# Hybrid attention layer on one core: the compressed branch for four heads at once, the gate product on GpSimd, 640-key scores cut as 384 + 256

## What is computed

```python
s = jnp.einsum('bqhgd,bihd->bhgqi', qblk, kc)            # compressed
valid = cmp_end[None, :] <= t[:, None]
p_cmp = jax.nn.softmax(jnp.where(valid, s, -1e30), axis=-1) * valid
o_cmp = jnp.einsum('bhgqi,bihd->bqhgd', p_cmp, vc)
...
p_slc = jax.nn.softmax(s.reshape(*s.shape[:4], n_sel * SLC_BLOCK), axis=-1).reshape(s.shape)
...
p_win = jax.nn.softmax(jnp.where(mw, s, -1e30), axis=-1)
...
o = g[..., 0:1] * o_cmp + g[..., 1:2] * o_slc + g[..., 2:3] * o_win
```

## Time and profile before

| | |
|---|---|
| time, median of 3 runs | 915.43 us (914.12 to 916.51) |
| the profiled execution | 917.05 us, span 915.2 us |
| TensorE busy, of the span | 855.7 us (93%) |
| VectorE | 516.7 us (56%) |
| ScalarE | 468.8 us (51%) |
| GpSimd | 364.0 us (40%) |

### The profile page before, as it was taken

One profiled execution on the slowest core, in us unless ns is written; L12 is line 12 of the kernel. 1 busy time (PEld: TensorE's weight loads), 2 busy tenths in 40 slices (PEclk: granted clock), 3 DMA queues, 4 the chain that ended last, 5 costly groups with the idle time before them and its releaser, 6 DMA issues.

```text
span 915.2 us, 12680 instructions
## 1 busy us (share of the span) xinstructions
PE 855.7 (93%) x4674; PEld 706.3 (77%) x4674; DVE 516.7 (56%) x1066; ACT 468.8 (51%) x1021; POOL 364.0 (40%) x302
## 2 busy tenths in 40 slices
PE   3999999999999999999889998999988999999994
PEld 3887798898888788777677876777767888887883
DVE  5301359281561704476978998899986026363434
ACT  5311343203232015768878897789976252625432
POOL 1311014517132121643336645254544446463563
PEclk9999979999999999999988999999999999999997
DMA  6342011201111010320000000000006723232339
GB/s 224 87 98 51 13 43 35 58 24 47 36 40 42 23 49 21 83 65 1 1 1 1 1 1 1 1 1 1 1 1 225 247 91 97 77 103 78 96 126 242
DMA packets 38397, 55.68 MB, mean 61 GB/s; under 512 B 11312, under 2 KB 17728, under 8 KB 38336
## 3 DMA queue, kind: packets, MB, share of 16 engines
q1 hardware_dynamic: 37616, 52.78, 19.1%
q0 software_dynamic: 720, 2.10, 1.3%
HBM read 48.58 MB, written 6.29 MB: 60 GB/s over the span
## 4 chain that ended last, share of the span: by engine, by line
PE 73%; DVE 16%; ACT 6%; issue 2%; DMA 1%; POOL 1%; SPq 0%; POOLq 0%; DVEq 0%; ACTq 0%
PE psum L718 47%; DVE pT_lo L1763 5%; PE psum L942 3%; PE psum L805 3%; PE psum L959 3%; PE psum L927 2%; PE psum L926 2%; DVE p_win L1740 2%; PE psum L960 2%; ACT pT_hi L1257 2%; PE psum L762 2%; DVE p_slc L1740 1%; PE psum L683 1%; DVE o_sum L1773 1%; DVE gla_z L1694 1%
## 5 line engine op out<-in xcount | busy, mean ns | idle before, releaser
L1374 POOL TENSOR_TENSOR w_lo<-w_raw,w_hi 128x512 fp32r<-128x512 f32 (+1 forms) x134 | 184.1, 1377 | 378.2 <-ACT w_hi L1065 377.7
L1065 ACT ACTIVATE w_hi<-w_raw 128x512 fp32r<-128x512 f32 (+1 forms) x134 | 82.9, 623 | 325.4 <-PE psum L718 304.5
L1763 DVE TENSOR_TENSOR pT_lo<-psum,pT_hi 128x512 fp32r<-128x512 f32 (+1 forms) x148 | 99.9, 685 | 13.7 <-ACT pT_hi L1257 13.0
L718 PE MATMUL psum<-w_hi,xT_hi 128*128 128x512 f32 x256 | 101.2, 395 | 1.7 <-DVE gla_state_b L1675 1.7
L1257 ACT ACTIVATE pT_hi<-psum 128x512 fp32r<-128x512 f32 (+1 forms) x148 | 86.3, 591 | 32.0 <-PE psum L942 31.3
L1406 POOL TENSOR_SCALAR p_slc<-p_slc,gate_over_sum 128x512 f32<-128x512 f32 (+7 forms) x40 | 66.7, 1678 | 85.4 <-DVE gate_over_sum L1749 85.4
L718 PE MATMUL psum<-w_hi,xT_lo 128*128 128x512 f32 x256 | 100.2, 391 | 0.0
L718 PE MATMUL psum<-w_lo,xT_hi 128*128 128x512 f32 x256 | 100.2, 391 | 0.0
L959 PE MATMUL psum<-pT_hi,v_hi_lo 128*128 128x512 f32 x132 | 62.0, 469 | 15.9 <-DVE pT_lo L1763 14.9
L926 PE MATMUL psum<-kT_hi_hi,qT_hi_lo 128*128 128x512 f32 (+3 forms) x192 | 70.9, 375 | 2.7 <-DVE neg_max L1740 2.5
L1248 ACT ACTIVATE p_slc<-p_slc,neg_max 128x512 f32<-128x512 f32 (+7 forms) x80 | 58.1, 728 | 8.8 <-DVE neg_max L1740 8.4
(11 more groups left out here) (261 smaller groups left out, 1961.3 us busy)
## 6 DMA issues: line engine op xcount, KB each, us to landing
w_raw<-in_w_in SPq DMA_DIRECT2D x56, 256.0 KB, 2.7
w_raw<-in_w_out SPq DMA_DIRECT2D x32, 256.0 KB, 2.7
w_raw<-in_ple_gate SPq DMA_DIRECT2D x32, 256.0 KB, 2.5
x_tok<-in_x SPq DMA_DIRECT2D x8, 512.0 KB, 7.0
h_tok<-in_x SPq DMA_DIRECT2D x8, 512.0 KB, 5.6
out<-h_tok SPq DMA_DIRECT2D x8, 512.0 KB, 5.7
w_raw<-in_ple_proj SPq DMA_DIRECT2D x8, 256.0 KB, 2.5
out<-out_tmp POOLq DMA_DIRECT2D x3, 512.0 KB, 5.6
```

Source lines behind the costliest of these rows:

```text
L718: mm = pe.matmul(out, lhs, rhs, start=(first and n == 0), stop=(final and n == 2))
L1065: act.activation(w_hi(i)[:, 0:w], raw[:, i % RAW, 0:w], ACT.Copy).then_inc(s_whi, 1)
L1374: pool.tensor_tensor(w_lo(i)[:, 0:w], raw[:, i % RAW, 0:w], w_hi(i)[:, 0:w].bitcast(F32), ALU.subtract).then_inc(s_wlo, 1)
L1763: dve.tensor_tensor(PTl[0:n, u % 4], bank(4 + u % TRING)[0:n], PTh[0:n, u % 4].bitcast(F32), ALU.subtract).then_inc(s_plo, 1)
```

## The change

The compressed step is no longer four heads one after the other:

- `KC1` and `KC2` become halves of one tile, so a head's scores are one matmul of 128 columns (64 of the high product, 64 of the low one), and four heads fill one bank (`compressed_scores`).
- `compressed_sum`, VectorE: a `tensor_reduce` over the two halves writes the scores of four heads to SBUF.
- `compressed_mask`, GpSimd, adds the mask; `compressed_max`, VectorE, makes the maxima of the four heads; `compressed_less_max`, GpSimd, subtracts them; `compressed_exponent`, ScalarE, is one exponential without a sum; VectorE sums in `gate_over_sum`; `compressed_scale`, GpSimd, is one product for the four heads.
- In all steps `gate_over_sum` is only the inversion, and the product with the gate is made on GpSimd (`gates`); all scalings wait for it.
- `scaler` of the selected branch is "APAP" for "VPAP".
- Scores of 640 keys lie from column 128 of a pair of banks, so they are cut 384 + 256.
- A compressed step uses the pairs of banks once and not four times (`events`, `bank_pair`, `pair_freed`).
- The planner has the new operations and other assumed durations (0.9 x keys for a score, 3.0 x keys for a scaling on GpSimd, where it had 0.83 and 3.6).

The diff, with "..." where lines are left out (declarations, the lists of kinds, the loops that call the new functions):

```diff
     PTl = sb("pT_lo", [P, 4, 512], F32R, R2 + 8192)
-    KC1 = sb("kcT_hi_hi", [P, NKV, 64], F32R, R6 + 7168)
-    KC2 = sb("kcT_lo_lo", [P, NKV, 64], F32R, R6 + 7680)
+    KC = sb("kcT_hi_lo", [P, NKV, 2, 64], F32R, R6 + 7168)
+    KC1, KC2 = KC[:, :, 0], KC[:, :, 1]
...
-    scaler = ("PPPP", "VPAP", "VPAP")
+    scaler = ("P", "APAP", "VPAP")
...
+    def bank_pair(s, g):
+        return event_of[s, g] % 2 * 2
...
+    def pair_freed(s, g):
+        return events[event_of[s, g] - 2] if event_of[s, g] >= 2 else None
...
+    def scores_at(s, g):
+        nk = span(*steps[s][1:])[1]
+        first = 128 if nk == 640 else 0
+        b = bank_pair(s, g)
+        return PSUM[:, b:b + 2].rearrange("p a b -> p (a b)")[:, first:first + nk], 512 - first
...
+            if step[2] == 0:
+                ops["cscore", s] = "P", 500, s
+                after["cscore", s] = after_pair(freed) + [("stack_lo", stacks_needed(step) - 1)]
+                for kind, eng, dur, *deps in (("csum", "V", 650, ("cscore", s), reuse), ("cmask", "G", 950, ("csum", s)),
+                                              ("cmax", "V", 400, ("cmask", s)), ("csub", "G", 950, ("cmax", s)),
+                                              ("cexp", "A", 550, ("csub", s)), ("gate", "V", 600, ("cexp", s)),
+                                              ("gates", "G", 400, ("gate", s)), ("cscale", "G", 950, ("gates", s))):
+                    ops[kind, s] = eng, dur, s
+                    after[kind, s] = deps
+                continue
...
-                ops["score", n] = "P", 0.83 * nk + 60, s
-                after["score", n] = [("mask_max", n - 2), ("stack_lo", stacks_needed(step) - 1)]
+                ops["score", n] = "P", 0.9 * nk + 60, s
...
-                ops["scale" + e, n] = e if e != "P" else "G", {"V": 0.6, "A": 0.83, "P": 3.6}[e] * nk + 150, s
-                after["scale" + e, n] = [("gate", s)]
-            ops["gate", s] = "V", 250, s
+                ops["scale" + e, n] = e if e != "P" else "G", {"V": 0.6, "A": 0.83, "P": 3.0}[e] * nk + 150, s
+                after["scale" + e, n] = [("gates", s)]
+            ops["gate", s] = "V", 180, s
             after["gate", s] = [("exponent", GRP * s + GRP - 1)]
+            ops["gates", s] = "G", 400, s
+            after["gates", s] = [("gate", s)]
...
+        def wait_pair(s, g):
+            freed = pair_freed(s, g)
+            if freed and steps[freed[0]][2]:
+                pe.wait_ge(s_ttr, masked_count(*freed))
+            elif freed:
+                pe.wait_ge(s_csum, compressed_count(freed[0]))
+        def compressed_scores(s):
+            kv, qt, _ = steps[s]
+            wait_pair(s, 0)
+            pe.wait_ge(s_qlo, stacks_needed(steps[s]))
+            for g in range(GRP):
+                mm = pe.matmul(bank(bank_pair(s, 0))[:, g * P:(g + 1) * P], QS[:, kv * GRP + g, qt * P:(qt + 1) * P],
+                               KC[:, kv].rearrange("p a j -> p (a j)"), start=True, stop=True)
+            mm.then_inc(s_cqk, 1)
         def scores(n):
             s, g = divmod(n, GRP)
             kv, qt, br = steps[s]
             k0, nk = span(qt, br)
-            if n >= 2:
-                pe.wait_ge(s_ttr, n - 1)
+            wait_pair(s, g)
             if g == 0:
                 pe.wait_ge(s_qlo, stacks_needed(steps[s]))
             lhs = QS[:, kv * GRP + g, qt * P:(qt + 1) * P]
-            for c0 in range(0, nk, 512):
-                w = min(512, nk - c0) if br else NCMP + 1
-                out = bank(n % 2 * 2 + c0 // 512)[:, 0:w]
-                if br == 0:
-                    kk = [KC1[:, kv], KC2[:, kv]]
-                else:
-                    ks = slice(k0 + c0, k0 + c0 + w)
-                    kk = [K1[:, (br - 1) * NKV + kv, ks], K2[:, (br - 1) * NKV + kv, ks]]
-                pe.matmul(out, lhs, kk[0], start=True, stop=False)
-                mm = pe.matmul(out, lhs, kk[1], start=False, stop=True)
+            out, cut = scores_at(s, g)
+            for c0, c1 in ((0, min(cut, nk)), (cut, nk)):
+                if c0 < c1:
+                    ks = slice(k0 + c0, k0 + c1)
+                    h = (br - 1) * NKV + kv
+                    pe.matmul(out[:, c0:c1], lhs, K1[:, h, ks], start=True, stop=False)
+                    mm = pe.matmul(out[:, c0:c1], lhs, K2[:, h, ks], start=False, stop=True)
             mm.then_inc(s_qk, 1)
...
             act.activation(probs(s)[:, g, 0:nk], probs(s)[:, g, 0:nk], ACT.Exp, bias=NM[:, n:n + 1],
                            scale=-1.0, accum_out=SU[:, n:n + 1]).then_inc(s_exp, 1)
+        def compressed_exponent(s):
+            act.wait_ge(s_csub, compressed_count(s))
+            x = probs(s)[:, :, 0:NCMP]
+            act.activation(x, x, ACT.Exp, scale=DH ** -0.5).then_inc(s_cexp, 1)
...
+        def compressed_mask(s):
+            qt = steps[s][1]
+            x, m0 = probs(s)[:, :, 0:NCMP], M_CMP + 7 * 8 - 8 * qt
+            pool.wait_ge(s_csum, compressed_count(s))
+            pool.tensor_tensor(x, x, MK[:, m0:m0 + NCMP].bitcast(BF16).unsqueeze(1).to_broadcast([P, GRP, NCMP]),
+                               ALU.add).then_inc(s_cmask, 1)
+        def compressed_less_max(s):
+            x = probs(s)[:, :, 0:NCMP]
+            pool.wait_ge(s_cmax, compressed_count(s))
+            pool.tensor_tensor(x, x, CMX[:, (s // 3) % 2].unsqueeze(2).to_broadcast([P, GRP, NCMP]),
+                               ALU.subtract).then_inc(s_csub, 1)
+        def gates(s):
+            kv, qt, br = steps[s]
+            n = slice(GRP * s, GRP * s + GRP)
+            pool.wait_ge(s_rcp, s + 1)
+            pool.tensor_tensor(RG[:, n], RG[:, n], GT[:, qt, kv * GRP:(kv + 1) * GRP, br], ALU.mult).then_inc(s_rg, 1)
+        def compressed_scale(s):
+            x = probs(s)[:, :, 0:NCMP]
+            pool.wait_ge(s_rg, s + 1)
+            pool.tensor_tensor(x, x, RG[:, GRP * s:GRP * s + GRP].unsqueeze(2).to_broadcast([P, GRP, NCMP]),
+                               ALU.mult).then_inc(s_norm, 1)
...
+        def compressed_sum(s):
+            ready_buffer(s)
+            dve.wait_ge(s_cqk, compressed_count(s))
+            v = bank(bank_pair(s, 0)).rearrange("p (g a j) -> p g j a", g=GRP, a=2)
+            dve.tensor_reduce(probs(s)[:, :, 0:NCMP], v[:, :, 0:NCMP], FREE, ALU.add).then_inc(s_csum, 1)
+        def compressed_max(s):
+            if s >= 6:
+                dve.wait_ge(s_csub, compressed_count(s) - 2)
+            dve.wait_ge(s_cmask, compressed_count(s))
+            dve.tensor_reduce(CMX[:, (s // 3) % 2], probs(s)[:, :, 0:NCMP], FREE, ALU.max).then_inc(s_cmax, 1)
...
             kv, qt, br = steps[s]
             n = slice(GRP * s, GRP * s + GRP)
-            dve.wait_ge(s_exp, GRP * (s + 1))
-            link(dve.reciprocal(RG[:, n], SU[:, n]))
-            dve.tensor_tensor(RG[:, n], RG[:, n], GT[:, qt, kv * GRP:(kv + 1) * GRP, br],
-                              ALU.mult).then_inc(s_rg, 1)
+            if br == 0:
+                dve.wait_ge(s_cexp, compressed_count(s))
+                dve.tensor_reduce(SU[:, n], probs(s)[:, :, 0:NCMP], FREE, ALU.add).then_inc(s_cadd, 1)
+                dve.wait_ge(s_cadd, compressed_count(s))
+            else:
+                dve.wait_ge(s_exp, masked_count(s, GRP - 1))
+            dve.reciprocal(RG[:, n], SU[:, n]).then_inc(s_rcp, 1)
```

More of the change, by code:

```diff
@@ L25 @@
 ACT = mybir.ActivationFunctionType
+FREE = mybir.AxisListType.X
 P = 128
@@ L314, in build_program @@
     s_rg = sem("gate_over_sum")
+    s_rcp = sem("sum_inverted")
+    s_cqk = sem("cmp_scores")
+    s_csum = sem("cmp_scores_summed")
+    s_cmask = sem("cmp_scores_masked")
+    s_cmax = sem("cmp_max_made")
+    s_csub = sem("cmp_max_taken")
+    s_cexp = sem("cmp_probs")
+    s_cadd = sem("cmp_probs_summed")
     s_norm = sem("probs_scaled")
@@ L449, in build_program, with masked_count, compressed_count @@
     first_unit.append(len(units))
-    scaler = ("PPPP", "VPAP", "VPAP")
+    scaler = ("P", "APAP", "VPAP")
+    events, event_of = [], {}
+    for s_, (kv_, qt_, br_) in enumerate(steps):
+        for g_ in range(GRP if br_ else 1):
+            event_of[s_, g_] = len(events)
+            events.append((s_, g_))
+    def masked_count(s, g):
+        return sum(1 for t, h in events[:event_of[s, g] + 1] if steps[t][2])
+    def compressed_count(s):
+        return s // 3 + 1
+    def bank_pair(s, g):
[7 more added lines that the diff above has]
+        return PSUM[:, b:b + 2].rearrange("p a b -> p (a b)")[:, first:first + nk], 512 - first
     def scaled_count(e, s):
@@ L527, in attention_timeline @@
             ops["turn", u] = "P", 430, s
-            after["turn", u] = [("scale" + scaler[steps[s][2]][g], GRP * s + g) for g in range(GRP)] \
-                + [("low", u - TRING), ("gate_mm", KD - 1), ("stack_lo", first_half - 1)]
+            after["turn", u] = ([("scale" + scaler[steps[s][2]][g], GRP * s + g) for g in range(GRP)]
```

(20 more changed lines are left out.)

47 lines of the change are left out of this document (29 added, 18 removed).

## The result

The changed kernel takes 902.06 us (median of 4 runs, 901.60 to 903.55) against 915.48 (4 runs, 914.12 to 916.51): a ratio of 0.9855, 95% interval 0.9839 to 0.9871, or 13.4 us less. I forecast 911.0 with a range of 902 to 921: the sign was right, the gain was three times what I had worked out. The profiled execution took 901.97 us with a span of 900.2.

What follows compares the result with a forecast made beforehand. No engine saturated: TensorE, VectorE and ScalarE near nine tenths busy, taking turns in the attention stage. Terms -3.9 (TensorE), -0.9 (VectorE), -0.3 (ScalarE), -1.2 and +1.9 (waits) sum to -4.4 us: 915.4 to 911.0, range 902 to 921.

Steps and rivals of the forecast that it cites:

- TensorE's terms: Compressed scores as four 128-column matmuls -7.2 us, 640-key scores as 384 + 256 -2.0; sum -9.2 us of TensorE work.
- VectorE's saving: Compressed steps +11.2 us, gate product gone from 32 other steps -3.5, selected scalings gone -10.0; net -2.3 us.
- GpSimd: too large: Three 252-element instructions per compressed step for four scalings, +9.6 us; gate product in 48 steps, +14.4; together +24 us.
- ScalarE: a little too small: One compressed exponential for four, -15.0 us; second scaling in selected steps, +11.7; net -3.3 us.
- wait (b): VectorE waiting for GpSimd before the compressed maximum, and for maximum, subtraction, exponential before its sum; costed at nothing.
- the last rival: Slower, 920 us (chance 0.20): VectorE held by GpSimd's 1.9 us scalings, deciding from 0.7 us a group.
- Wait (a): Every scaling waits about 0.3 us more for GpSimd's gate product; counted in 16 window steps, +1.9 us.
- The handovers term: Compressed scores pass a pair of banks once, not four times, a step: -2.4 us of waits, half counted, -1.2.
- The prices: Time per microsecond of work, from shares of the attention stage's chain of waits: TensorE 0.42, VectorE 0.40, ScalarE 0.10.
- The first rival: More gain, 905 us (chance 0.17): 1.2 GHz clock stretches near 470 and 485 us vanish, -5 us; handovers count fully.
- The second rival: No change, 915.5 us (chance 0.17): TensorE's gain turns into waiting for VectorE, whose work is the same.
- the third: GpSimd and VectorE fully block each other on a shared port: sixteen removed scalings worth -8 us more, 903 (chance 0.04).

Runs made afterwards that it cites:

- the small edits: Kernel before with gate product on GpSimd, APAP selected scaling, 384 + 256 split and new planner durations, compressed heads still one by one: 0.9924, -7.0 us.
- the fused branch: Changed kernel with gate product on VectorE, VPAP, 512 + 128 split and old planner durations, so only the compressed branch is fused: 0.9953, -4.3 us.

## Why the prediction was wrong in size

**TensorE's terms: right.** Timeline of TensorE in after:

```profile
487.56 0.34 PE L994 MATMUL psum<-kT_hi_hi,qT_hi_lo 128*128 128x384 f32 x1
...
488.15 0.39 PE L1027 MATMUL psum<-pT_hi,v_hi_lo 128*128 128x512 f32 x1
...
488.98 0.64 PE L977 MATMUL psum<-kcT_hi_lo,qT_hi_lo 128*128 128x128 f32 x4
489.46 0.44 PE L1027 MATMUL psum<-pT_hi,v_hi_lo 128*128 128x512 f32 x1
```

A 640-key head takes 488.15 - 487.56 = 0.59 us (I said 0.60), a compressed step 489.46 - 488.98 = 0.48 (I said 0.45). The -9.2 us stands within half a microsecond.

**VectorE's saving: larger than I said.** Timeline of VectorE in after:

```profile
485.65 0.18 DVE L1882 RECIPROCAL gate_over_sum<-exp_sum 128x4 f32<-128x4 f32 x1
485.77 0.82 DVE L1869 CUSTOM_DVE_ANT_0 p_win<-psum,masks 128x640 f32<-128x640 f32 x1
...
489.95 0.68 DVE L1852 TENSOR_REDUCE p_cmp<-psum 128x252 f32<-128x504 f32 x1
490.55 0.68 DVE L1895 TENSOR_TENSOR pT_lo<-psum,pT_hi 128x512 fp32r<-128x512 f32 x1
...
493.33 0.40 DVE L1858 TENSOR_REDUCE cmp_max<-p_cmp 128x4 f32<-128x252 f32 x1
493.65 1.08 DVE L1869 CUSTOM_DVE_ANT_0 p_slc<-psum,masks 128x896 f32<-128x896 f32 x1
...
496.56 0.41 DVE L1878 TENSOR_REDUCE exp_sum<-p_cmp 128x4 f32<-128x252 f32 x1
497.00 0.18 DVE L1882 RECIPROCAL gate_over_sum<-exp_sum 128x4 f32<-128x4 f32 x1
497.09 1.06 DVE L1869 CUSTOM_DVE_ANT_0 p_slc<-psum,masks 128x896 f32<-128x896 f32 x1
```

The add takes 0.60 us, so its strided read of PSUM costs nothing here. The maximum takes 0.32 and the sum with its wait 0.44. What I mis-sized is the inversion: I took 0.17 for it, the distance in which its successor was still the product that needs its result; followed by something independent it costs 0.09 to 0.12. A compressed step is 1.45 against 0.84, +9.8 instead of +11.2; the other 32 steps lose 0.16 to 0.19 each, 5.4 instead of 3.5; the scalings lose 12.5 - 2.1 = 10.4. Net -6.0 where I had -2.3 (by busy time it is -9.3).

**GpSimd: too large.** Groups of after, 430 to 680 us (busy us, mean ns, idle before):

```profile
L1479 POOL TENSOR_TENSOR p_cmp<-p_cmp,masks 128x252 f32<-128x252 f32 x14 | 9.4, 670 | 13.8 <-DVE p_cmp L1852 13.7
L1497 POOL TENSOR_TENSOR p_cmp<-p_cmp,gate_over_sum 128x252 f32<-128x252 f32 x15 | 9.1, 608 | 0.9
L1492 POOL TENSOR_TENSOR gate_over_sum<-gate_over_sum,gates 128x4 f32<-128x4 f32 x45 | 8.9, 202 | 89.2 <-DVE gate_over_sum L1882 89.1
```

The instructions of 252 elements take 0.61 to 0.67 us instead of 0.8, the gate product 0.20 instead of 0.3, at the low end of its bounds. GpSimd grew by 8.7 us over the span, not 24; that it stands at 57% of the stage, near the 60% I named, is partly because the stage is shorter.

**ScalarE: a little too small.** Timeline of ScalarE in after:

```profile
495.80 0.41 ACT L1324 ACTIVATE p_cmp<-p_cmp 128x252 f32<-128x252 f32 x1
496.11 1.05 ACT L1318 ACTIVATE p_slc<-p_slc,neg_max 128x896 f32<-128x896 f32 x1
```

The exponential of four heads takes 0.31 us where I took 0.39, so the net is about -4.6, not -3.3.

**Waits.** In the attention stage VectorE waited for GpSimd 0.3 us in all, before the compressed maximum:

```profile
L1858 DVE TENSOR_REDUCE cmp_max<-p_cmp 128x4 f32<-128x252 f32 x16 | 6.4, 399 | 0.3 <-POOL p_cmp L1479 0.3
```

So wait (b) at nothing was right, and the last rival (slower, from 0.7 us a group) was wrong: the cover that the planner puts in between holds. Wait (a), +1.9, is nowhere in the waits of VectorE (ScalarE's scalings waited 1.5 us for the product over the span, where they had waited 1.8 before), and putting the product back on VectorE made the kernel slower by 5.4 us, so the hop costs less than the 8.2 us of VectorE's work that it takes away. The handovers term, -1.2, fits the 2.4 us of TensorE's idle time before compressed scores that went.

**The prices: the step that failed.** I priced TensorE at 0.42, VectorE at 0.40 and ScalarE at 0.10, because the chain's shares are these. They add up to one at most by construction. Measured by added work they are 0.8 to 0.9 for TensorE, 0.56 for VectorE and 0.4 to 0.6 for ScalarE, together near two. The failure is clearest for TensorE, which has the largest term: -9.2 x 0.42 = -3.9 should have been about -7.8. ScalarE's 0.10 lies outside the interval in before and at its edge in after. VectorE's 0.40 is not refuted, since it lies inside 0.34 to 0.79, and 0.42 is left when the clock's part is taken off. Its term fell short by its size, -6.0 for -2.3.

With my own sizes the measured prices give -9.2 x 0.85 - 2.3 x 0.56 - 3.3 x 0.5 = -10.8 where I had -5.1; with VectorE's measured size, -7.8 - 3.4 - 1.7 = -12.9 (and -13.5 with ScalarE's -4.6), against -13.4 measured. That it comes so near is partly luck: the intervals of the prices allow -9.6 to -15.9, and neither the clock's 2.0 us nor my two wait terms are in it. Of the 9.0 us between -4.4 and -13.4 TensorE's price makes 3.9, the recovered clock 2.0, wait (a) 1.9, VectorE's size 3.7 x 0.40 = 1.5 and ScalarE's price 1.3: 10.6 together, more than is needed, but inside the same intervals. The same prices also give the halves: the small edits, with -2.0 on TensorE, -18.1 (7.7 + 10.4) on VectorE and +11.7 on ScalarE, -6.0 (measured -7.0); the fused branch, with -7.2, +12.8 (16 x (0.60 + 0.32 + 0.44 + 0.28 - 0.84)) and -15.0, -6.4 (-4.3, interval -6.4 to -2.2, so only at its edge). They fail for the scaling put back in after: 10.0 x 0.56 - 11.7 x 0.5 is nothing, and 8.1 was measured. There VectorE is busy 515.5 us and ScalarE 453.5, so the balance is lost, and VectorE's microsecond may be worth more than where the two are even; that is argued, not shown. The measured prices are slopes around one kernel, not constants.

Why they add up to more than one is argued, not shown piece by piece: a tile goes from TensorE to ScalarE to VectorE and back, with four transposed tiles in flight and the order of issue fixed, so a delay on any of the three engines reaches the others, and each microsecond counts at whichever of many near-equal paths is late.

**The first rival, the clock: a part of the gain that my sum put at nothing.** I had written that the forecast would be wrong at its root if the low stretches vanished, and both did in after. By the slope between executions that is worth 2.0 us, and 3.6 if all of the recovered work counted: less than the 5 that the rival had, and more than the sum's nothing. The other 11 us are there at equal clock, so the rival doesn't explain the gain. Either half of the change alone raises the mean clock as far (0.987 in both), so this part is in each of the two gains. What holds the clock up in them isn't shown. In the kernel with the scaling put back low stretches returned in part (0.66 and 0.75 in two stretches of 5 us); over its ten executions it loses 15.0 us to the clock where after loses 12.4, which at the slope is 1.5 of its 8.1.

**No change, and the port.** The second rival fell with the price of TensorE: its gain was not eaten by VectorE. For the third, the removed scalings are worth 8.1 us when put back, about what it had named, so the sum alone doesn't refute it; the timelines speak against it. My reading of the earlier trace rows in it was off: a blocked scaling would have begun near 561.7 and ended near 562.3, and it ended at 561.0. GpSimd and VectorE in after:

```profile
494.39 3.94 POOL L1504 TENSOR_SCALAR p_win<-p_win,gate_over_sum 128x640 f32<-128x640 f32 x2
```
```profile
495.35 0.55 DVE L1889 TENSOR_SCALAR p_win<-p_win,gate_over_sum 128x640 f32<-128x640 f32 x1
```

VectorE's scaling began about 1 us into GpSimd's first of 1.97 and took the 0.55 of an undisturbed one. The longest of the eight scalings of 640 elements took 1.09, never the length of a wait for a GpSimd scaling. The Trainium skill ("SBUF — State Buffer", Who interferes with whom) has the second of the two fully blocked when VectorE's is in a two-port mode; here it wasn't, and at 559.98 us of before it was delayed by 0.5 us. Spans on GpSimd are rough, so how the delay arises stays open.

## What to carry to other kernels

Where several engines are nine tenths busy and hand tiles round in a ring with a fixed order, don't price a microsecond by an engine's share of the chain of waits: here TensorE's was worth 0.8 to 0.9 where its share said 0.42, and ScalarE's some 0.5 where it said 0.10. Add a few microseconds of unused work to each engine in turn and take the slopes, and trust them only while the balance holds. Moving small instructions and whole rows of work to an engine that idles four tenths of the time paid, since other work covered each hop. And compare the granted clock over many executions of each kernel before a clock theory is kept or dropped on one profile.
